# Attention block of a three-layer kernel: where the row factor of the input norm is multiplied in

## The chip, the cores and the metric

The kernel runs on one core of a Trainium2 chip. A core has five engines with a queue of instructions each, which run in order and wait for one another through semaphores: TensorE (PE, matrix products into the accumulator memory PSUM; the load of its stationary operand is listed as PEld), VectorE (DVE), ScalarE (ACT), GpSimd (POOL) and SyncE (SP, which here issues the DMAs). The metric is the device time of one execution in microseconds (us), the median over several runs. A profile is one further execution, taken with the hardware profiler.

## What is computed

Three transformer layers over 256 tokens of width 1024. The part that the change touches is the second norm of the first layer and the attention behind it, in the reference:

```python
x = x + FFN_RESIDUAL * rmsnorm(swiglu(rmsnorm(x, g[0]), ffn_w_in[i, 0], ffn_w_out[i, 0]), g[1])
h = rmsnorm(x, g[2])
...
m = diff_attention(h, attn_w_qkv[j], attn_w_o[j], attn_lam[j], attn_subln_g[j], rel_bias, lambda_init)
...
x = x + rmsnorm(m, g[3])
```

`rmsnorm(x, g)` is x times g (a weight per column) times the row factor 1/sqrt(mean of x squared + 1e-6), one number per token. `diff_attention` projects h to queries, keys and values, with 8 heads of 128 columns.

## The kernel before

**Data.** X, the residual stream, lies in SBUF with tokens on partitions, in two halves h = 0 and 1 of 128 tokens. A linear layer needs its input with columns on partitions, so the normed half `xn` is turned: eight PE transposes of 128x128 a half (`transposed`, line 2279), four to a PSUM bank. Products run in two-part precision: each operand is split into a rounded high part and the remainder. For the turned input ACT copies PSUM to `xhi` (`evict_hi`, line 822) and DVE subtracts to get `xlo` (`evict_lo`, line 1447). For weights, SP loads 1 MB pairs of units into `raw`, ACT writes `whi` (line 747), DVE writes `wlo` (line 1325). A unit is 128x1024 and four units are split at a time, so that `whi` of unit u waits until PE has used unit u-4. Each product is made of three: high times high, high times low, low times high (all on line 2134, where `mm` is).

**The place.** Unit 65 is the last of the first feed-forward layer (`ffn(0)`). Units 66 to 69 are the value weights `v0` of heads 0 to 3, units 70 and 71 the query and key weights of head 0, 72 and 73 those of head 1, and so on.

Between `ffn(0)` and `v0` the norm is settled, in an order that is written out by hand for each engine (`take_turns` with `ORDER_DEFER`, six steps for h = 0 woven with six for h = 1). For each half: ACT squares the layer's output with a row sum (`squares`, 787); POOL makes its row factor `r1` (610, 615); DVE multiplies by the weights g1 (1395, 1402) and adds to X (`add_x`, 1422); ACT squares X with a row sum (`squares2`, 814); POOL makes the second row factor `r2`; DVE writes `xn` = X times r2 times g2 (`norm`, 1430). Then PE turns `xn`. While PE waits it runs products whose result is not used: `fill_in` and `turn_idle`, twelve ahead of the first turn (`meanwhile`) and four ahead of the second, which stands in the middle of the v0 products of half 0 (`values`).

**Attention.** Head after head, PE runs the two query and key units (24 products each), the scores, the transposes of the softmax weights and the product with the values. The steps of different heads are interleaved by fixed lags (`head_at`). For each head, ACT takes queries and keys out of PSUM (`query_key`, 988 and 989), takes the exponential (964) and turns up again for three smaller steps; DVE adds the bias and takes the maximum (1593, 1596), weights the two softmaxes (1601 to 1612), scales the head's output (1620) and makes its low part (1626). All of that stands in the queues between the splits of the weight units (747, 1325).

Of the kernel before, what the change touches and what calls it, by code (L numbers as in the profile page):

```python
# [8 lines left out]
S = 256  # L9
# [22 lines left out]
DEFER = (1,)  # L32
# [3 lines left out]
FOLDED = STARTS + GATES  # L36
# [78 lines left out]
def n_sq(k, h, i=None):  # L115

    n = N_SQ1[k]
    if k in DEFER:
        return n_sq_first(k, h, i)
    i = n + 1 if i is None else i  # L120
    return n_sq_first(k, 0, 0) + (h * n + i if i < n else n + 2 * h + i)
# [64 lines left out]
def program(nc, w, rows, cols, pT, b1c, ssm_s, ssm_b, ssm_c, ssm_cc, oh, idn, eo, x, out, scr):  # L186
# [4 lines left out]
    with ctx:  # L191
# [85 lines left out]
        s_g8, s_vv, s_lam, s_lexp, s_qk = (sem(n) for n in ("s_g8", "s_vv", "s_lam", "s_lexp", "s_qk"))  # L277
# [67 lines left out]
        g8 = b1t[:, 128:256]  # L345
        lam, le = stat(4), stat(2)
# [256 lines left out]
        def gpsimd(g):  # L603
# [27 lines left out]
            def settle(k):  # L631
                if k in FOLDED or k == STORED:
# [100 lines left out]
        def scalar(a):  # L733
# [251 lines left out]
            def query_key(h):  # L985
                b = 4 + h % 2
                q.wait_ge(s_used, ATTN_AT + QK_AT[h] + 2)
                a.activation(turned(q_t[:, h, :]), in128(PS[:, b, 0:S]), ACT.Copy, scale=0.125)
                a.activation(k_t[:, h, :], PS[:, b, S:2 * S], ACT.Copy).then_inc(s_qk, 1)

            def values(name, bank, cols, out):
                for h in range(2):
# [4 lines left out]
                    a.activation(vv[:, h, out], PS[:, bank + h, cols], ACT.Copy).then_inc(s_vv, 1)  # L997

            def attention():
                def heads(j):  # L1000
                    for h in head_at(j, 4):
                        turned_weights(h)
                    for h in head_at(j, 0):
                        query_key(h)
# [7 lines left out]
                linear("v0", 4, head=4, tail=0, finish=lambda: evict_hi(1, 1))  # L1012
# [270 lines left out]
            settle(1, {1: lambda: released(0)})  # L1283
# [28 lines left out]
        def vector(v):  # L1312
# [91 lines left out]
            def add_x(k, h):  # L1404
# [12 lines left out]
                for i, f in enumerate((LO, HI)):  # L1417
# [4 lines left out]
                    v.scalar_tensor_tensor(X[:, h, f], src[:, f], by, X[:, h, f], MUL, ADD).then_inc(s_X, 1)  # L1422

# [203 lines left out]

            def attention():
                def heads(j):
                    for h in head_at(j, 6):  # L1630
                        head_normed(h)
# [10 lines left out]
                for j in range(4, 30):  # L1642
                    heads(j)
# [450 lines left out]
            take_turns(1, steps, {2: lambda: released(0)})  # L2094
# [34 lines left out]
        def tensor(pe):  # L2129
# [109 lines left out]
            def meanwhile(k, h):  # L2239
                b = tr_bank(k, h, 0)  # L2240
                if h and k not in DEFER:
# [8 lines left out]
                if k not in DEFER:  # L2250
                    turn_idle(k, b, s_X, n_x(k, 1, 1), 8 if k == PLACED else 4)

            def transposed(k, h):
# [3 lines left out]
                if k not in FOLDED and not (h and k in DEFER):  # L2257
                    meanwhile(k, h)
# [189 lines left out]
            def scores(h):  # L2448
                q.wait_ge(s_qk, h + 1)
# [32 lines left out]
            def attention():  # L2482
                def values(name, cols, bank, ns, last, by_half=None):
# [3 lines left out]
                    for h in range(2):  # L2487
# [614 lines left out]
```

## Time and profile before

| | us |
|---|---|
| median of 3 runs (1666.51 to 1667.78) | 1667.3 |
| the profiled execution | 1664.28 |
| its span, first to last instruction | 1662.5 |
| PE busy in the span | 1632.9 |
| DVE busy | 1101.2 |
| ACT busy | 927.6 |
| POOL busy | 165.8 |

PE is busy 98% of the span, but that counts the products whose result is not used. The settling of the attention's norm lies between 196 and 219 us of the span, the eight heads up to about 304 us. In the rows below a time such as 203.80 is in us from the start of the span.

### The profile page before, as it was taken

What the parts mean: (1) busy time and instruction counts of PE and PEld (TensorE: products, weight loads), DVE (VectorE), ACT (ScalarE), POOL (GpSimd) and SP (SyncE); (2) the same over time, 40 slices, a digit from 0 to 9 for tenths busy, and PEclk for the clock granted to TensorE, in tenths of its full rate; (3) what the DMA queues carried; (4) which work ended last, traced back from release to release, by engine and by line L of the source; (5) the groups of instructions that cost most, each with busy time, mean ns of one, the idle gap of its engine ahead of it and who ended that gap; (6) DMA issues with size and microseconds to landing.
All of it is one profiled execution on the core that took longest, in us unless ns stands there. A gap on an engine that the chain in (4) does not pass through costs nothing.

```text
span 1662.5 us, 22547 instructions
## 1 busy us (share of the span) xinstructions
PE 1632.9 (98%) x8995; PEld 1372.6 (83%) x8995; DVE 1101.2 (66%) x1567; ACT 927.6 (56%) x1559; POOL 165.8 (10%) x240
## 2 busy tenths in 40 slices
PE   9999999999999999999999999999999999999997
PEld 7888899788888877888878888788889889788886
DVE  5555667788877664869775556755567776665555
ACT  6555556655567585452465556655555444655555
POOL 0000001128301111900000000000000000000000
PEclk9999999999999999999999999999999999999999
DMA  6765443555555544451555545565544333554552
GB/s 235 252 209 186 181 165 127 179 195 191 189 191 190 206 174 152 174 181 52 190 184 182 198 178 190 192 219 199 179 176 178 140 116 128 184 203 177 196 184 102
DMA packets 50297, 295.93 MB, mean 178 GB/s; under 512 B 6072, under 2 KB 12688, under 8 KB 16528
## 3 DMA queue, kind: packets, MB, share of 16 engines
q1 hardware_dynamic: 49744, 293.86, 49.4%
q8 instruction: 71, 1.16, 0.3%
q0 software_dynamic: 160, 0.52, 0.1%
q14 instruction: 34, 0.28, 0.1%
q10 hardware_dynamic: 288, 0.11, 0.0%
HBM read 293.39 MB, written 1.09 MB: 177 GB/s over the span
## 4 chain that ended last, share of the span: by engine, by line
PE 89%; DVE 5%; ACT 4%; issue 1%; POOL 0%; DMA 0%; POOLq 0%; DVEq 0%; ACTq 0%
PE PS L2134 84%; PE PS L2356 2%; DVE wlo L1325 1%; PE PS L2279 1%; PE PS L2137 1%; ACT SC L964 1%; ACT whi L747 1%; PE PS L2571 0%; ACT wk L787 0%; DMA raw<-in_w 0%; DVE SC L1910 0%; DVE SC L1612 0%; DVE st L1596 0%; ACT wk L814 0%; DVE SC L1593 0%
## 5 line engine op out<-in xcount | busy, mean ns | idle before, releaser
L1331 DVE SCALAR_TENSOR_TENSOR wlo<-raw,ct,whi 128x512 fp32r<-128x512 f32 (+1 forms) x552 | 425.1, 815 | 259.2 <-ACT whi L751 259.2
L2134 PE MATMUL PS<-whi,xhi 128*128 128x512 f32 (+1 forms) x1312 | 505.6, 395 | 6.0 <-DVE wlo L1331 2.2
L751 ACT ACTIVATE whi<-raw,ct 128x512 fp32r<-128x512 f32 (+1 forms) x552 | 377.5, 734 | 224.2 <-PE PS L2134 170.6
L2134 PE MATMUL PS<-wlo,xhi 128*128 128x512 f32 (+1 forms) x1312 | 495.5, 387 | 0.0
L1325 DVE TENSOR_TENSOR wlo<-raw,whi 128x1024 fp32r<-128x1024 f32 x240 | 296.6, 1244 | 215.9 <-ACT whi L747 215.5
L2134 PE MATMUL PS<-whi,xlo 128*128 128x512 f32 (+1 forms) x1312 | 405.5, 387 | 0.0
L747 ACT ACTIVATE whi<-raw 128x1024 fp32r<-128x1024 f32 x240 | 251.8, 1057 | 258.4 <-PE PS L2134 192.1
L2134 PEld LDWEIGHTS PS<-whi,xhi 128*128 128x128 f32 x1312 | 246.0, 188 | 60.9 <-ACT xhi L822 4.1
L2134 PEld LDWEIGHTS PS<-whi,xlo 128*128 128x128 f32 x1312 | 246.4, 188 | 51.4
L2134 PEld LDWEIGHTS PS<-wlo,xhi 128*128 128x128 f32 x1312 | 246.6, 188 | 47.4
L2134 PE MATMUL PS<-whi,hhi 128*128 128x512 f32 x544 | 173.3, 392 | 0.1
L2134 PE MATMUL PS<-wlo,hhi 128*128 128x512 f32 x544 | 171.9, 389 | 0.0
L2134 PE MATMUL PS<-whi,hlo 128*128 128x512 f32 x544 | 171.6, 389 | 0.0
L610 POOL TENSOR_SCALAR st<-st 128x1 f32<-128x1 f32 x42 | 14.4, 343 | 1139.6 <-ACT wk L787 592.2
L2134 PE MATMUL PS<-xhi,whi 128*128 128x256 f32 x416 | 119.8, 289 | 0.0
L2134 PEld LDWEIGHTS PS<-whi,hlo 128*128 128x128 f32 x544 | 102.1, 188 | 21.4
L2134 PEld LDWEIGHTS PS<-wlo,hhi 128*128 128x128 f32 x544 | 102.1, 188 | 21.3
L2134 PEld LDWEIGHTS PS<-whi,hhi 128*128 128x128 f32 x544 | 101.0, 188 | 20.8 <-issue 0.7
L2134 PE MATMUL PS<-xhi,wlo 128*128 128x256 f32 x416 | 117.3, 283 | 0.0
L2134 PE MATMUL PS<-xlo,whi 128*128 128x256 f32 x416 | 116.4, 283 | 0.0
L881 ACT ACTIVATE wk<-PS,st 128x256 f32<-128x256 f32 x132 | 60.7, 470 | 41.4 <-PE PS L2134 40.6
L2134 PEld LDWEIGHTS PS<-xhi,whi 128*128 128x128 f32 x416 | 79.6, 191 | 1.6 <-issue 0.4
(282 smaller groups left out, 1508.7 us busy)
## 6 DMA issues: line engine op xcount, KB each, us to landing
raw<-in_w SPq DMA_DIRECT2D x263, 1024.0 KB, 4.8
gr<-in_rows SPq DMA_DIRECT2D x14, 512.0 KB, 3.9
SC<-scratch SPq DMA_DIRECT2D x5, 512.0 KB, 5.7
X<-in_x SPq DMA_DIRECT2D x2, 512.0 KB, 5.1
raw<-in_w SPq DMA_DIRECT2D x2, 512.0 KB, 6.7
SC<-scratch SPq DMA_DIRECT2D x4, 256.0 KB, 5.1
xn<-in_sc SPq DMA_DIRECT2D x2, 512.0 KB, 6.1
SC<-scratch SPq DMA_DIRECT2D x1, 1024.0 KB, 8.8
```

What stands on the lines that cost most here:

```text
L610: g.tensor_scalar(ms, ss[:, 0:1], ss[:, 1:2], eps, ADD, ADD).then_inc(s_ms, 1)
L747: a.activation(hi, src, ACT.Copy).then_inc(s_hi, 1)
L751: e = a.activation(hi[:, f], src[:, f], ACT.Copy, scale=ct[:, c:c + 1])
L881: a.activation(sg[:, h, :], PS[:, up_bank(n, j) + h, 0:S], ACT.Silu, scale=r2[k][h]).then_inc(s_silu, 1)
L964: e = a.activation(pr[:, m, l:z], sc[:, m, l:z], ACT.Exp, bias=n4[:, m, c:c + 1], accum_out=s4[:, m, c:c + 1])
L1325: v.tensor_tensor(lo, src, hi.bitcast(f32), SUB).then_inc(s_lo, 1)
L1331: e = v.scalar_tensor_tensor(lo[:, f], src[:, f], ct[:, c:c + 1], hi[:, f].bitcast(f32), MUL, SUB)
L2134: return pe.matmul(o, l, r, start=start, stop=stop)
L2137: return pe.matmul(o, l, r, start=False, stop=True, skip_group_check=True)
L2279: e = pe.transpose(PS[:, tr_bank(k, h, kq), 128 * i:128 * i + 128], src[:, h, 128 * (4 * kq + i):128 * (4 * kq + i) + 128], idt[:, :])
L2356: e = pe.transpose(PS[:, turn_bank(n), at:at + 128], hf[:, h, 128 * i:128 * i + 128], idt[:, :])
```

## The change

The row factor r2 is no longer multiplied into `xn`. What is turned is X times the weights g2 alone, and r2 is multiplied in later: into the values when ACT takes them out of PSUM (tokens are on partitions there, so r2 is ACT's scale per partition), and into queries and keys, where tokens are along the free axis and a row of factors is needed that is the same on all partitions. For that, DVE multiplies a 128x128 identity by r2 of each half (`factors`), PE transposes the two, DVE copies the result into `rk`, and `query_key`, which moves from ACT to DVE, multiplies by `rk` as it leaves PSUM. The idle products of this norm are gone. Half 1 is turned after all v0 products of half 0 rather than in their middle. `squares2` of both halves moves on ACT behind the eviction of half 1.

```diff
 def settle(k):
-    if k in FOLDED or k == STORED:
+    if k in FOLDED + DEFER or k == STORED:
...
-def query_key(h):
-    b = 4 + h % 2
-    q.wait_ge(s_used, ATTN_AT + QK_AT[h] + 2)
-    a.activation(turned(q_t[:, h, :]), in128(PS[:, b, 0:S]), ACT.Copy, scale=0.125)
-    a.activation(k_t[:, h, :], PS[:, b, S:2 * S], ACT.Copy).then_inc(s_qk, 1)
...
-        a.activation(vv[:, h, out], PS[:, bank + h, cols], ACT.Copy).then_inc(s_vv, 1)
+        q.wait_ge(s_r2, n_one(1, h))
+        a.activation(vv[:, h, out], PS[:, bank + h, cols], ACT.Copy, scale=r2[1][h]).then_inc(s_vv, 1)
...
+    def turned_1():
+        evict_hi(1, 1)
+        squares2(1, 0)
+        squares2(1, 1)
-    linear("v0", 4, head=4, tail=0, finish=lambda: evict_hi(1, 1))
+    linear("v0", 4, head=4, tail=0, finish=turned_1)
...
-settle(1, {1: lambda: released(0)})
+squares(1, 0)
+released(0)
+squares(1, 1, (0,))
+evict_hi(1, 0, (0,))
+squares(1, 1, (1,))
+use(ATTN_AT - 1)
+evict_hi(1, 0, (1,))
+use(ATTN_AT)
 attention()
...
+def add_x_times_g2(k, h):
+    q.wait_ge(l_x[h], 16)
+    q.wait_ge(s_r1, n_r1(k, h))
+    q.wait_ge(s_yg, n_yg(k, h))
+    g2 = row_in(ROW_G2[k])
+    for i, f in enumerate((LO, HI)):
+        v.scalar_tensor_tensor(X[:, h, f], yg_of(k, h)[:, f], r1[k][h], X[:, h, f], MUL, ADD).then_inc(s_X, 1)
+        q.wait_ge(s_X, n_x(k, h, i))
+        v.tensor_tensor(xn[:, h, f], X[:, h, f], g2[:, f], MUL).then_inc(s_xn, 1)
...
+def factors():
+    q.wait_ge(s_tr, n_tr(1, 1))
+    for h in range(2):
+        q.wait_ge(s_r2, n_one(1, h))
+        v.tensor_scalar(xn[:, h, 768:896], idt[:, :], 0.0, r2[1][h], MUL, ADD).then_inc(a_rk, 1)
+
+def query_key(h):
+    if h == 0:
+        q.wait_ge(a_rkT, 1)
+        v.tensor_copy(rk, PS[:, 2, 0:S].rearrange("p (h t) -> p h t", h=2)).then_inc(a_rk, 1)
+        q.wait_ge(a_rk, 3)
+    q.wait_ge(s_used, ATTN_AT + QK_AT[h] + 2)
+    b = PS[:, 4 + h % 2, :]
+    v.scalar_tensor_tensor(turned(q_t[:, h, :]), in128(b[:, 0:S]), 0.125, rk, MUL, MUL)
+    v.tensor_tensor(in128(k_t[:, h, :]), in128(b[:, S:2 * S]), rk, MUL).then_inc(a_key, 1)
...
 for j in range(4, 30):
+    if j == 5:
+        factors()
     heads(j)
...
-take_turns(1, steps, {2: lambda: released(0)})
+gate_or_low(1, 0)
+times_g(1, 0)
+add_x_times_g2(1, 0)
+released(0)
+evict_lo(1, 0, (0,))
+gate_or_low(1, 1)
+times_g(1, 1)
+use(ATTN_AT - 1)
+evict_lo(1, 0, (1,))
+use(ATTN_AT)
+add_x_times_g2(1, 1)
 attention()
...
-                if k not in FOLDED and not (h and k in DEFER):
+                if k not in FOLDED + DEFER:
                     meanwhile(k, h)
...
+                        if h and by_half is not None:
+                            transposed(1, 1)
-                            if low is False and h == 0 and n == 2:
-                                fill_in(tr_bank(1, 1, 0), ATTN_AT, 4)
-                                transposed(1, 1)
...
                 values("v0", slice(0, 512), 0, range(4), True, 1)
+                q.wait_ge(a_rk, 2)
+                for h in range(2):
+                    e = pe.transpose(PS[:, 2, 128 * h:128 * h + 128], xn[:, h, 768:896], idt[:, :])
+                e.then_inc(a_rkT, 1)
```

In the orders that follow, `PS` is PSUM, `PS<-whi` alone is a product whose result is not used, `SC` the scratch that holds queries, keys and softmax, `gr` the rows of norm weights, `idt` the identity. On PE, between the last product of `ffn(0)` and the first of v0, before:

```order
L2134 MATMUL PS<-whi,hlo 128x512
L2134 MATMUL PS<-whi 128x512 [waits s_lo,s_sq]
L2134 MATMUL PS<-whi 128x512 x3
L2134 MATMUL PS<-whi 128x512 [waits s_r1]
L2134 MATMUL PS<-whi 128x512 x3
L2134 MATMUL PS<-whi 128x512 [waits s_X]
L2134 MATMUL PS<-whi 128x512 x3
L2279 MATMUL PS<-idt,xn 128x128 [waits s_xn,s_vec]
L2279 MATMUL PS<-idt,xn 128x128 x3
L2279 MATMUL PS<-idt,xn 128x128 [waits s_xn]
L2279 MATMUL PS<-idt,xn 128x128 x3
L2134 MATMUL PS<-whi,xhi 128x512 [waits s_xhi]
```

And now:

```order
L2179 MATMUL PS<-whi,hlo 128x512
L2323 MATMUL PS<-idt,xn 128x128 [waits s_xn,s_vec]
L2323 MATMUL PS<-idt,xn 128x128 x3
L2323 MATMUL PS<-idt,xn 128x128 [waits s_xn]
L2323 MATMUL PS<-idt,xn 128x128 x3
L2179 MATMUL PS<-whi,xhi 128x512 [waits s_lo,s_xhi]
```

The twelve idle products are gone, and the turn of half 0 stands right behind the feed-forward layer.

On PE, between the last v0 product and the first query and key unit, before:

```order
L2134 MATMUL PS<-whi,xhi 128x512
L2134 MATMUL PS<-wlo,xhi 128x512
L2134 MATMUL PS<-whi,xlo 128x512
L2134 MATMUL PS<-xhi,whi 128x256 [waits s_lo]
L2134 MATMUL PS<-xlo,whi 128x256
```

And now:

```order
L2179 MATMUL PS<-whi,xlo 128x512
L2567 MATMUL PS<-idt,xn 128x128 [waits a_rk]
L2567 MATMUL PS<-idt,xn 128x128
L2179 MATMUL PS<-xhi,whi 128x256 [waits s_lo]
L2179 MATMUL PS<-xlo,whi 128x256
```

The two transposes of the factors are new there, with a wait for DVE's `factors`.

On DVE, from the end of the settling to the first head, before:

```order
L1447 TENSOR_TENSOR xlo<-PS,xhi 128x4x128 [waits s_xhi] x2
L1430 SCALAR_TENSOR_TENSOR xn<-X,st,gr 128x512 [waits s_r2]
L1430 SCALAR_TENSOR_TENSOR xn<-X,st,gr 128x512
L1640 TENSOR_SCALAR b1t<-b1t 128x128 [waits l_b1]
L1325 TENSOR_TENSOR wlo<-raw,whi 128x1024 [waits s_hi] x2
L1447 TENSOR_TENSOR xlo<-PS,xhi 128x4x128 [waits s_xhi] x2
L1325 TENSOR_TENSOR wlo<-raw,whi 128x1024 [waits s_hi] x6
```

And now:

```order
L1435 SCALAR_TENSOR_TENSOR X<-PS,st,X 128x512
L1437 TENSOR_TENSOR xn<-X,gr 128x512 [waits s_X]
L1673 TENSOR_SCALAR b1t<-b1t 128x128 [waits l_b1]
L1462 TENSOR_TENSOR xlo<-PS,xhi 128x4x128 [waits s_xhi] x2
L1330 TENSOR_TENSOR wlo<-raw,whi 128x1024 [waits s_hi] x4
L1647 TENSOR_SCALAR xn<-idt,st 128x128 [waits s_r2,s_tr]
L1647 TENSOR_SCALAR xn<-idt,st 128x128 [waits s_r2]
L1330 TENSOR_TENSOR wlo<-raw,whi 128x1024 [waits s_hi]
L1652 COPY xn<-PS 128x2x128 [waits a_rkT]
L1656 SCALAR_TENSOR_TENSOR SC<-PS,xn 128x2x128 [waits s_used,a_rk]
```

The two low parts of units 68 and 69 now stand further ahead, in the settling, and `factors` stands behind the low parts of units 70 to 73.

## Rows read from the trace of the kernel before

**Rows 1.** Waits of PE, whole span: waiter, releaser, us in total, times, longest.

```profile
PE PS L2819 <- DVE SC L2007: 3.6, 2, 1.9
...
PE PS L2465 <- DVE SC L1612: 0.8, 1, 0.8
PE PS L2465 <- DVE hlo L1626: 0.6, 1, 0.6
```

**Rows 2.** PE's timeline, 200 to 220: start, us, instruction, count, idle before, releaser.

```profile
200.35 2.88 PE L2134 MATMUL PS<-whi 128*128 128x512 f32 x12
203.80 1.23 PE L2279 MATMUL PS<-idt,xn 128*128 128x128 f32 x8 [0.57 <-DVE xn L1430]
...
208.95 1.32 PE L2279 MATMUL PS<-idt,xn 128*128 128x128 f32 x8
210.88 0.50 PE L2134 MATMUL PS<-whi,xhi 128*128 128x512 f32 x1 [0.61 <-DVE wlo L1325]
...
219.39 0.28 PE L2134 MATMUL PS<-xhi,whi 128*128 128x256 f32 x1
```

**Rows 3.** DVE's timeline in the same stretch.

```profile
198.44 1.41 DVE L1422 SCALAR_TENSOR_TENSOR X<-PS,st,X 128x512 f32<-128x512 f32 x2 [0.40 <-POOL st L615]
...
208.14 1.41 DVE L1430 SCALAR_TENSOR_TENSOR xn<-X,st,gr 128x512 f32<-128x512 f32 x2 [1.31 <-POOL st L615]
...
209.61 2.35 DVE L1325 TENSOR_TENSOR wlo<-raw,whi 128x1024 fp32r<-128x1024 f32 x2
...
219.38 2.52 DVE L1325 TENSOR_TENSOR wlo<-raw,whi 128x1024 fp32r<-128x1024 f32 x2 [0.19 <-ACT whi L747]
```

**Rows 4.** ACT's timeline in the same stretch.

```profile
204.46 1.20 ACT L822 ACTIVATE xhi<-PS 128x512 fp32r<-128x512 f32 x2 [2.19 <-PE PS L2279]
205.55 0.62 ACT L814 ACTIVATE wk<-X 128x512 f32<-128x512 f32 x1
...
206.36 0.63 ACT L814 ACTIVATE wk<-X 128x512 f32<-128x512 f32 x1
...
206.99 1.99 ACT L747 ACTIVATE whi<-raw 128x1024 fp32r<-128x1024 f32 x2
...
219.59 1.06 ACT L747 ACTIVATE whi<-raw 128x1024 fp32r<-128x1024 f32 x1 [0.24 <-PE PS L2134]
```

**Rows 5.** PE's timeline inside the heads: two small transposes and the product behind them.

```profile
251.37 0.44 PE L2479 MATMUL PS<-idt,xn 128*128 128x128 f32 x2
251.56 0.36 PE L2134 MATMUL PS<-xhi,whi 128*128 128x256 f32 x1
```

**Rows 6.** ACT's timeline inside the heads: queries and keys, twice.

```profile
255.42 0.38 ACT L988 ACTIVATE SC<-PS 128x256 f32<-128x256 f32 x1
255.68 0.39 ACT L989 ACTIVATE SC<-PS 128x256 f32<-128x256 f32 x1
...
286.38 0.39 ACT L988 ACTIVATE SC<-PS 128x256 f32<-128x256 f32 x1 [1.02 <-PE PS L2134]
```

**Rows 7.** DVE's timeline inside the heads, one head of the steady run.

```profile
257.13 0.60 DVE L1620 SCALAR_TENSOR_TENSOR xn<-PS,st,b1t 128x128 f32<-128x128 f32 x2
258.97 1.23 DVE L1325 TENSOR_TENSOR wlo<-raw,whi 128x1024 fp32r<-128x1024 f32 x1 [1.23 <-ACT whi L747]
```

**Rows 8.** DVE instructions from PSUM by line: ns min/median/max, first and last start, forms.

```profile
L1509 DVE SCALAR_TENSOR_TENSOR wk<-PS,st,wk x132: 466/479/486, 28.1 to 1613.6; 128x256 f32<-128x256 f32 x132
...
L1626 DVE TENSOR_TENSOR hlo<-PS,hhi x4: 412/414/417, 253.8 to 277.6; 128x256 fp32r<-128x256 f32 x4
```

**Rows 9.** PE's timeline at the start and at the end of the span.

```profile
1.04 5.49 PE L2134 MATMUL PS<-rot 128*128 128x128 f32 x24 [1.04 <-DVE rot L2089]
...
7.59 2.84 PE L2134 MATMUL PS<-rot 128*128 128x128 f32 x24
...
1653.05 0.39 PE L2134 MATMUL PS<-whi,xlo 128*128 128x512 f32 x1
```

**Rows 10.** Stretch, its length, busy PE, PEld, DVE, ACT, POOL; granted clock, DMA share, GB/s.

```profile
1655.50:1656.00 0.50, 0.00 (x0) 0.00 (x0) 0.50 (x1) 0.41 (x2) 0.29 (x1) 0.74 0.00 0
```

More of the change, by code:

```diff
@@ L117, in n_sq @@
     n = N_SQ1[k]
-    if k in DEFER:
-        return n_sq_first(k, h, i)
     i = n + 1 if i is None else i
@@ L276, in program @@
         s_phi, s_plo, s_prj, s_gate, s_gated = (sem(n) for n in ("s_phi", "s_plo", "s_prj", "s_gate", "s_gated"))
-        s_g8, s_vv, s_lam, s_lexp, s_qk = (sem(n) for n in ("s_g8", "s_vv", "s_lam", "s_lexp", "s_qk"))
+        a_rk, a_rkT, a_key = (sem(n) for n in ("a_rk", "a_rkT", "a_key"))
+        s_g8, s_vv, s_lam, s_lexp = (sem(n) for n in ("s_g8", "s_vv", "s_lam", "s_lexp"))
         a_sc, a_add, a_max, a_exp, a_rc, a_at, a_pt, a_aT, a_av, a_sq, a_r, a_on, a_xt, a_oh, a_ol = (
@@ L345, in program @@
         g8 = b1t[:, 128:256]
+        rk = xn[:, :, 896:1024]
         lam, le = stat(4), stat(2)
@@ L1002, in heads @@
                         turned_weights(h)
-                    for h in head_at(j, 0):
-                        query_key(h)
                     for h in head_at(j, 7):
@@ L1626, in head_lo @@
                 v.tensor_tensor(lo, PS[:, o_bank(h), 0:S], hi.bitcast(f32), SUB).then_inc(a_ol, 1)
+            def factors():
[12 more added lines that the diff above has]
+                v.tensor_tensor(in128(k_t[:, h, :]), in128(b[:, S:2 * S]), rk, MUL).then_inc(a_key, 1)
             def attention():
                 def heads(j):
+                    for h in head_at(j, 0):
+                        query_key(h)
                     for h in head_at(j, 6):
@@ L2240, in meanwhile @@
                 b = tr_bank(k, h, 0)
-                if h and k not in DEFER:
+                if h:
                     if k == PLACED:
@@ L2249, in meanwhile @@
                 turn_idle(k, b, s_X, n_x(k, h, 1), 9 if k == PLACED else 4)
-                if k not in DEFER:
-                    turn_idle(k, b, s_X, n_x(k, 1, 1), 8 if k == PLACED else 4)
+                turn_idle(k, b, s_X, n_x(k, 1, 1), 8 if k == PLACED else 4)
             def transposed(k, h):
@@ L2448, in scores @@
             def scores(h):
-                q.wait_ge(s_qk, h + 1)
+                q.wait_ge(a_key, h + 1)
                 if h:
@@ L2528, in attention @@
                     if h >= 2:
-                        q.wait_ge(s_qk, h - 1)
+                        q.wait_ge(a_key, h - 1)
                     for n in range(2):
@@ L2535, in attention @@
                     heads(22 + n)
-                q.wait_ge(s_qk, 8)
+                q.wait_ge(a_key, 8)
                 linear("wo", o_place, 4, tail=2, step=-2, ready=lambda k: q.wait_ge(a_ol, k + 1),
```

## The prediction, made before the changed kernel was run

> **What bounds the kernel now.** I read the waits of PE first. In the whole attention only two waits of PE are worth naming, both at the turn of a head's softmax weights: 0.8 us behind DVE L1612 and 0.6 us behind DVE L1626 [rows 1]. Elsewhere in the heads PE runs without a gap, so PE's own time is the bound there, and what the change can win lies at the settling of the norm. There I read the timelines of three engines side by side. PE is free of the feed-forward layer at 200.35, runs idle products, waits for xn, turns half 0 at 203.80, half 1 at 208.95, waits again until 210.88 for a low part of weights, and starts the first query and key unit at 219.39 [rows 2]: 19.0 us. Of that, 48 v0 products are real work; the 36 from 210.88 to 219.39 take 8.51 us, 0.236 each, some 11 us for all, and the two turns take 2.6 [rows 2]. So some 5.4 us are waiting or idle products. The price is the chain X, squares, r2 on POOL, then xn: DVE stands 1.31 us for r2 even at half 1 [rows 3].
>
> **The change part by part.** I follow the new orders with the durations of the rows, in the old span's time.
>
> Half 0. X starts at 198.44 as before, since r1 is unchanged. Two X halves back to back take 1.41 [rows 3], one alone some 0.74. The new X times g2 on 128x512 is not in the trace; it lies between half of a 128x1024 subtraction (2.35/2/2 = 0.59) and one of the L1430 pair (0.70) [rows 3]; I take 0.65, nearer the form with two tensors. With the wait for its own X each pair costs some 1.45, so the second half of xn is done at 201.3 and PE has turned half 0 at 202.1. Before, that was 203.80 + 1.23 = 205.0 [rows 2]. Gain so far 2.9 us.
>
> DVE then becomes the bound, since everything stands in one queue: low part of unit 67 (1.17), xlo (0.65), two multiplications by g1 (0.65 each), low part of unit 68 (1.17), xlo (0.65), low part of unit 69 (1.17): 201.3 + 6.1 = 207.4. PE needs unit 69 for the last quarter of half 0 and ends that at some 209.3. X and xn of half 1 take 2.9 more on DVE: 210.2. The turn of its second bank (0.65), ACT's xhi (1.20/2 = 0.60 [rows 4]) and xlo bring PE to 211.4, and 24 products of half 1 end at 216.9. Before it was 219.39 [rows 2]. Gain 2.5 us, with 1.5 to 3.3 as bounds, by how many of the nine DVE steps overlap.
>
> The factors. Here the change adds a wait that the diff hardly shows. PE's two new transposes stand ahead of the first query and key unit and wait for `factors`; `factors` stands on DVE behind the low parts of units 70 to 73; unit 73 needs ACT's high part, and that waits until PE has used unit 69, the last v0 unit. So PE waits for something that only begins when PE has finished. Before, ACT took unit 73 at 219.59, 0.20 after v0 ended, and DVE ended its low part at 219.38 + 2.52 = 221.90, 2.51 after it [rows 3, 4]; nobody waited for that. Two `factors` add some 0.36 and the start of PE 0.14: at least 3.0 us.
>
> It is more, since ACT comes late: behind the eviction of half 1 (211.4) stand four `squares2`, 0.81 each by their starts (206.36 - 205.55), 3.2 us, and then four high parts at 1.0 [rows 4]: 211.4 + 3.2 + 4.0 = 218.6. DVE follows: first low part from 215.7, four at 1.17, 220.4, `factors` 220.7, PE 220.9. The transposes cost 0.19 (251.37 to 251.56) and some 0.1 on the product behind them [rows 5]. First unit at 221.1 instead of 219.39: the settling is **1.7 us slower**, not faster; bounds +0.8 and +2.5. Behind the waiting transposes stands all of PE's work.
>
> The r2 that values and factors need is there by some 215.8 and holds nobody. SP passes its wait for the last xn at some 210.2 instead of 209.5 and its next weight pair is wanted at 216.6, so the loads stay hidden. Values with a scale cost ACT nothing that PE sees.
>
> Queries and keys. ACT loses 0.65 us per head (255.42 to 256.07) [rows 6]. DVE gains one multiplication like L1509, 0.48, and one like L1626, 0.41 [rows 8], some 0.8 back to back, 6.4 for eight heads. In the steady head DVE is done with L1620 at 257.73 and stands 1.23 us until ACT's high part releases 258.97 [rows 7]. The 0.8 stand right in front of L1620, so that gap hides them, with 0.4 to spare. If the cover were gone, each head would cost up to 0.8. A page bears on this: the Trainium skill, VectorE: DVE Perf Modes, Specifications, says that VectorE sits closer to SBUF and ScalarE closer to PSUM, which speaks against moving a PSUM read to DVE. The rows show little of it, 0.41 and 0.48 on DVE against 0.38 and 0.39 on ACT [rows 6, 8], and the sum goes by the rows.
>
> What the heads give back. The 0.6 us at L2465 came from a loop of ACT and DVE (exponential, high part, low part, softmax weights, bias, maximum) that ran as tight as PE. With PE 1.7 us later against it and ACT shorter, that wait should go. The 0.8 us came from ACT standing 1.02 us for the queries of the last head ahead of an exponential [rows 6]; with DVE doing those, the exponential starts some 0.6 earlier and 0.15 of the wait is left. Together **-1.2 us**, bounds 0 and -1.4. What is late next is PE itself.
>
> The clock. The wait of PE at the factors is some 3.9 us (216.9 to 220.9), and the idle products that used to fill this settling are gone. The longest waits of PE inside the trace are 1.9 us [rows 1], and no stretch of the work shows the granted clock below full. At the end, PE's last product ends at 1653.44 and the granted clock falls from 1.0 (2.4 GHz) to half in the middle of 1655.5 to 1656.0, 2.3 us later [rows 9, 10]. So a wait of 3.9 us is past what PE got away with and past what it did not. What a fall costs I bound by the start of the span: 24 idle products took 5.49 us there and the next 24 took 2.84 [rows 9]: 0 to 2.65 us lost, and I take 1.4, the middle. The Trainium skill, TensorE: Matmul & The Clock Gate, HAM oscillation, says the same in general: gaps in PE's work throttle it to half rate, and it has to be busy again before it is released. By that page alone the fall would be counted in full, and the sum would be its upper end, +3.2; this trace shows the fall once, at the end, and the return only by the durations at the start.
>
> **Sum** against the profiled 1664.28: +1.7 - 1.2 = +0.5 if the clock holds, 1664.8; +1.9 with the fall, 1666.2. The median of the runs stands 3.0 above the profiled execution; carried over, 1667.8 and 1669.2.
>
> **The rivals.** What a measurement here can tell from no change is about 0.2%, 3.3 us.
> (a) Forecast: the wait at the factors eats the gain and the clock falls: +1.9, 1669.2. For it: 3.9 us of wait against 2.3 us at the end. Against it: the fall needs to meet the wait, and I have one instance.
> (b) The same with the clock held: +0.5, 1667.8. For it: all waits inside the trace passed without a fall. Against it: they were half as long.
> (c) Slower beyond 0.2%: DVE becomes the bound of the heads. Place: DVE between L1620 and the low part of the even unit, gap 1.23 against 0.8 [rows 7]. It decides once the query and key pair takes over 1.23, say from the reversed write of queries, or if the 0.4 to spare is used up by late units; then the loop of ACT and DVE lengthens by up to 0.8 a head, 6.4 in all, less the 1.2 not given back: with (a), +3 to +8, 1672 as its middle. Against it: both forms are in the rows at half the gap.
> (d) Faster: the wait at the factors is short because v0 ends late or ACT early, and the gain of the settling is at its upper bound: -3.3 + 3.2 - 1.4 = -1.5 at best as a sum of rows, and beyond -3.3 only if the transposes didn't wait. The order says that they do. 1665.8 for the first, 1663 for the second.
>
> **How the numbers follow.** (a) 0.48, (b) 0.35, (c) 0.10, (d) 0.07, of which 0.05 go beyond -3.3. The likeliest is (a): 1669.2. The range takes (a) and (b) with their bounds: lowest +0.8 - 1.4 without a fall, -0.6, and some 1 us for the spread of the runs (1666.51 to 1667.78): 1665.7; highest +2.5 + 2.65 less 0.6 of the give-back, +4.5: 1671.8; what lies outside is most of (c) and half of (d). Faster 0.05; slower 0.13, (c) and a corner of (a); same 0.82.
>
> **What would show it.** Right: PE's first turn in attention ends near 202, v0 ends near 217, then PE idles 3 to 4 us with DVE's L1647 as releaser; the granted clock is below 1 in a few us around 221; in the heads L2465 no longer waits, and DVE's gap ahead of the even low part shrinks to some 0.4. Wrong: PE waits in every head behind DVE L1656 or L1657 (c); no wait at L2567 (d); the clock at 1.00 throughout (b).

## The result, and the profile after

The changed kernel takes 1667.25 us (median of 21 runs), the kernel before takes 1664.54 beside it (21 runs): ratio 1.0016, 95% interval 1.001 to 1.0021, some 2.7 us slower. That is within the 0.2% that the prediction counts as no change, and near its forecast of +1.9. The kernel before is 2.8 us quicker here than in the three runs from which the prediction started (1667.3; they are among the 21, and among the slower ones), so differences are compared below, not times. The profiled execution of the changed kernel is the slowest of its runs (1669.09, span 1667.3); what stands in its trace is not all typical, and a second profile is used beside it. One execution of a later run (factors first), at 2330 us, was a slow one and is left out of its ratio and of the counts below.

TensorE's timeline at the settling, as in [rows 2] (start, us, instruction, count, idle before, releaser):

```profile
201.16 0.66 PE L2323 MATMUL PS<-idt,xn 128*128 128x128 f32 x4 [0.41 <-DVE xn L1437]
201.57 0.48 PE L2179 MATMUL PS<-whi,xhi 128*128 128x512 f32 x1
...
205.31 0.47 PE L2179 MATMUL PS<-whi,xhi 128*128 128x512 f32 x1 [0.74 <-DVE wlo L1330]
...
206.95 0.50 PE L2179 MATMUL PS<-whi,xhi 128*128 128x512 f32 x1 [0.47 <-DVE wlo L1330]
...
211.03 0.47 PE L2179 MATMUL PS<-whi,xhi 128*128 128x512 f32 x1 [0.64 <-ACT xhi L822]
...
216.36 0.39 PE L2179 MATMUL PS<-whi,xlo 128*128 128x512 f32 x1
220.51 0.44 PE L2567 MATMUL PS<-idt,xn 128*128 128x128 f32 x2 [3.76 <-DVE xn L1647]
220.70 0.36 PE L2179 MATMUL PS<-xhi,whi 128*128 128x256 f32 x1
```

Half 0 is turned at 201.8 where it was 205.0, and the last v0 product starts at 216.36. Then TensorE stands for 3.76 us, the longest wait of its whole trace (the two transposes at 220.51), and the first query and key unit starts at 220.70 where it was 219.39. (The feed-forward layer ends at 200.15 here and 200.35 there, so 0.2 comes on top.) What it waits for is seen on ScalarE and VectorE, whose timelines answer to [rows 4] and [rows 3]. ScalarE:

```profile
213.98 1.99 ACT L747 ACTIVATE whi<-raw 128x1024 fp32r<-128x1024 f32 x2
216.61 2.00 ACT L747 ACTIVATE whi<-raw 128x1024 fp32r<-128x1024 f32 x2 [0.64 <-DMA raw<-in_w]
```

VectorE:

```profile
215.05 2.36 DVE L1330 TENSOR_TENSOR wlo<-raw,whi 128x1024 fp32r<-128x1024 f32 x2 [3.32 <-ACT whi L747]
217.70 2.36 DVE L1330 TENSOR_TENSOR wlo<-raw,whi 128x1024 fp32r<-128x1024 f32 x2 [0.28 <-ACT whi L747]
219.97 0.48 DVE L1647 TENSOR_SCALAR xn<-idt,st 128x128 f32<-128x128 f32 x2
```

The factors (L1647) stand on VectorE behind four low parts, and these follow four high parts that ScalarE begins at 213.98. The second pair of them waits 0.64 us for its load.

In a steady head VectorE now has the queries and keys (L1656, L1657) in the gap of [rows 7], and 0.57 us of the gap is left:

```profile
257.80 0.42 DVE L1656 SCALAR_TENSOR_TENSOR SC<-PS,xn 128x256 f32<-128x256 f32 x1
258.13 0.41 DVE L1657 TENSOR_TENSOR SC<-PS,xn 128x256 f32<-128x256 f32 x1
258.46 0.60 DVE L1635 SCALAR_TENSOR_TENSOR xn<-PS,st,b1t 128x128 f32<-128x128 f32 x2
259.64 1.23 DVE L1330 TENSOR_TENSOR wlo<-raw,whi 128x1024 fp32r<-128x1024 f32 x1 [0.57 <-ACT whi L747]
```

Among TensorE's waits there is none of the kind of [rows 1] at L2465 any more.

**Where the time goes, place by place.** For each profile I took the end of the feed-forward layer on TensorE (the row behind its last product: 200.35 before, 200.15 after) as zero, and from its timeline the start of the first query and key unit and of four later rows that every kernel has. Two of these rows, of after and then of before:

```profile
324.17 0.50 PE L2179 MATMUL PS<-whi,xhi 128*128 128x512 f32 x1 [0.25 <-ACT xhi L822]
...
802.81 0.73 PE L2179 MATMUL PS<-whi,xhi 128*128 128x512 f32 x2 [0.46 <-DVE xlo L1827]
```

```profile
324.12 0.50 PE L2134 MATMUL PS<-whi,xhi 128*128 128x512 f32 x1 [0.25 <-ACT xhi L822]
...
801.62 0.73 PE L2134 MATMUL PS<-whi,xhi 128*128 128x512 f32 x2 [0.45 <-DVE xlo L1792]
```

So at 324 the changed kernel is (324.17 - 200.15) - (324.12 - 200.35) = 0.25 us behind, at 802 it is 1.39 behind. The table gives that difference from the kernel before for all profiles of the study, in us (plus is later). The names of the runs are explained with the experiments.

| profile | first query unit, 220 | end of attention, 324 | 802 | 1308 | 1437 |
|---|---|---|---|---|---|
| before again | 0.00 | -0.02 | -0.17 | -0.17 | -0.17 |
| after | +1.51 | +0.25 | +1.39 | +1.41 | +5.02 |
| after again | +1.77 | +2.04 | +3.15 | +3.15 | +3.30 |
| turn later (e1) | -2.64 | -3.21 | -2.10 | -2.08 | +0.21 |
| factors first (e6) | -2.47 | -3.34 | -2.26 | -2.22 | -0.33 |
| idle in wait (e4) | +1.67 | +0.44 | +0.33 | +0.32 | +1.84 |
| idle in wait again | +1.55 | +0.30 | +0.15 | +0.16 | +0.12 |
| code only (e9) | +2.89 | +2.86 | +2.78 | +3.68 | +3.66 |
| factors first, padded (e8) | -2.47 | -3.18 | -3.21 | -3.18 | -1.67 |
| e8 again | -2.51 | -3.30 | -3.19 | -3.19 | -0.40 |
| idle in sliding (e11) | -2.49 | -3.17 | -3.26 | -2.60 | +1.61 |
| three idle (e12) | -2.51 | -3.35 | -3.34 | -3.35 | -3.35 |
| before, three idle (e13) | +0.02 | 0.00 | -0.09 | -0.14 | -0.18 |

Read the row of after from left to right: 1.5 us behind at the settling, 1.26 of it given back in the heads, then 1.1 us lost between 324 and 802, in code that the change does not touch, and 3.6 us lost in the third layer. Of these 3.6, 2.8 lie on two stretches at half clock behind 1309 and 1365, and 0.8 on a late load at 1435. The attention alone does not explain the result. What follows asks for each of these steps whether it belongs to the change.

### The profile page after: what moved, and what is told of

The parts are those of the page before. It is cut to its first block, busy times and chain, and to the rows that moved or that the text cites. A ratio compares the mean times of both kernels' runs of the same rounds, so it can differ in the third digit from the quotient of the medians.

```text
span 1667.3 us, 22526 instructions
## 1 busy us (share of the span) xinstructions
PE 1633.2 (98%) x8981; PEld 1372.5 (82%) x8981; DVE 1105.8 (66%) x1586; ACT 923.0 (55%) x1543; POOL 165.7 (10%) x240
## 3 DMA queue, kind: packets, MB, share of 16 engines
q8 instruction: 71, 1.16, 0.3%
## 4 chain that ended last, share of the span: by engine, by line
PE 89%; DVE 5%; ACT 3%; DMA 2%; issue 1%; POOL 0%; POOLq 0%; DVEq 0%; ACTq 0%; SPq 0%
PE PS L2179 84%; DMA raw<-in_w 2%; PE PS L2400 2%; DVE wlo L1330 1%; PE PS L2182 1%; PE PS L2323 1%; DVE wlo L1336 1%; ACT whi L747 1%; PE PS L2618 0%; ACT wk L787 0%; DVE SC L1945 0%; ACT whi L751 0%; DVE SC L1948 0%; ACT xhi L822 0%; DVE SC L2115 0%
```

## The experiments

All edits are in the changed kernel unless it is said otherwise. Ratios are to the kernel before, run beside it; they stand as the record gives them and can differ from the quotient of two medians by 0.0005.

### Is the factors' wait on the path? (e1, e6) And which losses come again? (two second profiles)

Turn later, on TensorE:

```diff
-q.wait_ge(a_rk, 2)
-for h in range(2):
-    e = pe.transpose(PS[:, 2, 128 * h:128 * h + 128], xn[:, h, 768:896], idt[:, :])
-e.then_inc(a_rkT, 1)
 for h in range(8):
+    if h == 1:
+        q.wait_ge(a_rk, 2)
+        for m in range(2):
+            e = pe.transpose(PS[:, 2, 128 * m:128 * m + 128], xn[:, m, 768:896], idt[:, :])
+        e.then_inc(a_rkT, 1)
```

> TensorE turns the two factors of the keys only after head 0's two query/key units, instead of ahead of them; nothing else is changed. Theory A (the 3.76 us of idle ahead of the first of these transposes in the changed kernel lie on the path that sets the end): the idle row with the releaser L1647 goes or falls under 0.3 us, the first query/key unit starts near 216.9 us of the span instead of 220.7, and the time falls by 3 to 3.9 us against the changed kernel, so to 1.0 to 1.6 us under the kernel before (ratio 0.9992). Theory B (the attention is held by VectorE or ScalarE and the wait only moves on): the first unit starts earlier, but its second or the scores wait for most of it, and the time stays within 1 us of the changed kernel (ratio 1.0010 to 1.0020).

Factors first, on VectorE:

```diff
 for j in range(4, 30):
-    if j == 5:
+    if j == 4:
         factors()
```

> VectorE makes the factors of the keys one slot earlier, ahead of the low parts of the last four weight units of the values; the order on TensorE stays. Theory A (VectorE's factors come late only because they stand behind those low parts in its order): the idle of TensorE ahead of the two small transposes falls from 3.76 to about 0.2 us, and the time falls by about 3.5 us against the changed kernel (ratio to before 0.9995). Theory B (the factors come late since their sums of squares come late from ScalarE, at 213.9 us): the idle stays above 2 us or moves to the first query/key unit, which then waits for the low parts, and the time falls by under 1.5 us (ratio 1.0007 or more).

Turn later takes 1663.45 us, ratio 0.9996 (0.9987 to 1.0005); factors first 1664.22, ratio 1.0004 (0.9994 to 1.0013); the changed kernel beside them 1667.22. Both are theory A: 3.0 to 3.8 us less by the medians, 3.5 and 3.6 at the end of the attention by the table. In factors first the two instructions run ahead of the low parts, and TensorE doesn't wait at all. VectorE, then TensorE:

```profile
212.50 0.29 DVE L1647 TENSOR_SCALAR xn<-idt,st 128x128 f32<-128x128 f32 x1 [1.84 <-POOL st L615]
214.05 0.29 DVE L1647 TENSOR_SCALAR xn<-idt,st 128x128 f32<-128x128 f32 x1 [1.26 <-POOL st L615]
214.25 4.77 DVE L1330 TENSOR_TENSOR wlo<-raw,whi 128x1024 fp32r<-128x1024 f32 x4
```

```profile
215.27 0.39 PE L2179 MATMUL PS<-whi,xlo 128*128 128x512 f32 x1
215.50 0.38 PE L2567 MATMUL PS<-idt,xn 128*128 128x128 f32 x2
```

The row factors are there at 214.05, in an idle time of VectorE. So what made the wait was the place of `factors` behind the low parts of units 70 to 73, not when the factors could be made.

> The changed kernel once more, for a second profile and more times. If the 2.7 us of the medians' difference are the attention's own, the alignment of TensorE's products with the kernel before shows +2.5 us or more at the end of the attention. If they come from the third layer (two stretches of some 3.4 us at granted clock 0.5, near 1311 and 1366 us, and loads that land late near 696 and 1431 us), the attention shows +0.3 us again, and the same stretches are there again at the same places. If these were of one execution alone, they are at other places or absent, and the span is 3 to 4 us shorter than 1667.3.

> The kernel before once more, for a second profile. If stretches at granted clock 0.5 in the third layer belong to the changed kernel, there are none ahead of 1655 us here, as in the first profile of it (span 1662.5). If they belong to an execution, not to a kernel, they can appear here too, and the span is longer by 1.2 to 1.7 us for each.

The second profile of the changed kernel (1667.22 us, ratio 1.0018, 1.0009 to 1.0027) decides between the steps. The 1.1 us between 324 and 802 are there again (from +2.04 to +3.15), and in turn later and factors first too (from -3.21 to -2.10, from -3.34 to -2.26): they come with the change. Of the 3.6 us of the third layer only 0.15 are there. Instead the attention ends at +2.04 rather than +0.25, for TensorE's granted clock, of which the first profile shows nothing there (stretch, its length, busy time, granted clock, DMA share, GB/s; first after, then after again):

```profile
219.00:220.50 1.50, 0.00 (x0) 1.00 0.86 350
220.50:222.00 1.50, 1.49 (x13) 1.00 1.00 393
```

```profile
219.50:220.00 0.50, 0.40 (x4) 0.99 0.97 410
220.00:223.00 3.00, 3.00 (x17) 0.50 0.92 360
```

In the second profile the transposes come after 4.02 us of idle, and from 220 to 223.5 the products run at granted clock 0.50, that is 1.2 GHz: 17 in 3 us where 13 took 1.5. With after's give-back of 1.26 the end of the attention would be at +0.51; it is at +2.04, so the fall costs 1.5 us. The profiles of before show no such stretch ahead of the end, in either (that this does not hold for all executions of before is seen at the end of the experiments).

### What is late between 324 and 802? (e4, e9)

The place is one load of weights in the first layer's second feed-forward. ScalarE waits for it. Its timeline before:

```profile
690.64 2.01 ACT L747 ACTIVATE whi<-raw 128x1024 fp32r<-128x1024 f32 x2 [4.24 <-DMA raw<-in_w]
```

After, where the same step starts 1.56 us later:

```profile
692.20 2.01 ACT L747 ACTIVATE whi<-raw 128x1024 fp32r<-128x1024 f32 x2 [5.74 <-DMA raw<-in_w]
```

TensorE, 5 us further on, waits for what follows from it; before, it has no wait there:

```profile
697.27 0.70 PE L2179 MATMUL PS<-whi,hhi 128*128 128x512 f32 x2 [0.83 <-DVE hlo L1530]
```

The load is issued at 685.9 before and 686.0 after, and lands 4.7 us later before and 6.2 after. The difference stands in the DMA queues. This is the view of the queues before, from 683 to 686, when no load is moving (queue, packets, MB, share of 16 engines):

```profile
q8 instruction: 1, 0.02, 2.1%
```

and after, from 686 to 692 (first the busy share of the 16 DMA engines in 40 slices):

```profile
DMA  0000009900000999999999999990300000101000
...
q1 hardware_dynamic: 144, 1.05, 54.4%
q8 instruction: 1, 0.02, 1.0%
```

Queue q8 brings code: 71 packets, 1.16 MB in the span, against 0.28 MB on q14, and TensorE has 17,962 of the 22,526 instructions (products and weight loads), so q8 is most likely TensorE's. Before, the packet comes at 684.6, between two loads. After, TensorE has 14 products and their 14 weight loads fewer, the packet comes at 689.4 and takes 0.93 us on one of the 16 DMA engines, in the middle of the load's transfer. A few packets of the load end late: see the three stray marks behind the block of nines. That they are the share of the DMA engine that carried the code is my reading; the view doesn't tell the 16 engines apart. The Trainium skill, Runtime: NRT & Kernel Launch, Instruction fetch mechanics, says that code comes in blocks of 16 KiB and that crossing one is mostly hidden. The size agrees (1.16 MB in 71), and TensorE itself runs on without a gap around 689.4. What pays is the load that the packet meets.

To test it, idle in wait gives TensorE 14 products back, where they cost no time:

```diff
+fill_in(3, ATTN_AT + 4, 14)
 q.wait_ge(a_rk, 2)
 for h in range(2):
     e = pe.transpose(PS[:, 2, 128 * h:128 * h + 128], xn[:, h, 768:896], idt[:, :])
```

> Into the changed kernel's wait for the two factor transposes (3.76 and 4.02 us in its two profiles) go 14 idle products of TensorE (128x512, 0.23 us each, 3.2 us in all), about as many as the change took out ahead of the first turn; the rest stays. Two theories on what makes the changed kernel 2.7 us slower at the median while its attention alone shows +0.24 us where the granted clock holds. Code theory: with 28 instructions fewer on TensorE, its code (fetched in packets of 16 KB) arrives at other times, and the packet at 689.4 us of the span, 0.93 us long, falls into the transfer of a weight load and holds one of its 16 parts back (landing 1.4 us late, TensorE idle 0.83 us at 697 us, +1.1 us in each profile of the three kernels that have the change); with the 28 instructions given back the packet moves to about 685 to 686, ahead of that load's transfer, the idle at 697 goes, and the time falls by about 1.1 us. Clock theory: the idle wait also drops the granted clock in part of the executions (half clock from 219.8 to 223.4 us in one of the two profiles, +1.5 us); with the idle products it holds there, and the median falls by up to 1.5 us more. Both together: ratio to before 1.0000 to 1.0007. If neither holds: 1.0014 to 1.0020, with the idle at 697 us still there.

> The changed kernel with the 14 idle products in its wait once more, for a second profile: if the idle products hold the clock, no half clock between 219 and 224 us again, and TensorE's idle at 697 us is absent again, since the code is the same.

Measured: 1665.11 us, ratio 1.0000 (0.9991 to 1.0009), and once more 1665.14, 1.0000 (0.9990 to 1.0010). The lag behind the kernel before is gone. For the code's part of it the mechanism named is seen. The view of the queues from 683 to 686 has the code packet again:

```profile
q8 instruction: 1, 0.02, 2.4%
```

ScalarE's high part comes at its old place,

```profile
690.15 2.01 ACT L747 ACTIVATE whi<-raw 128x1024 fp32r<-128x1024 f32 x2 [4.42 <-DMA raw<-in_w]
```

TensorE has no wait at L1530 in this stretch, and from 324 to 802 the table shows -0.11 and -0.15 instead of +1.1. Only TensorE's queue was edited, so the load's delay hangs on TensorE's instruction count. All 14 profiles bear this out. In the time of the kernel before (the packet's time less the lag at 324 and the shift of the zero) the packet stands at 688.8 to 689.4 in the four that lose the 1.1 us (after twice, turn later, factors first) and at 684.4 to 685.2 in the ten that don't. The clock held at 220 in both profiles of idle in wait.

The same is there once more in the third layer. ScalarE, before and then after:

```profile
1427.66 2.01 ACT L747 ACTIVATE whi<-raw 128x1024 fp32r<-128x1024 f32 x2 [4.25 <-DMA raw<-in_w]
```

```profile
1432.97 2.01 ACT L747 ACTIVATE whi<-raw 128x1024 fp32r<-128x1024 f32 x2 [5.58 <-DMA raw<-in_w]
```

The code packet that comes at 1420.8 before comes in the same time at 1426.2 after and 1426.5 in turn later, into the load, and TensorE loses 0.8 us in each from 1431 to 1437. In factors first and after again it comes at 1423.7, and the loss is 0.46 and 0.12. None of the other profiles loses anything there. So the count of instructions costs the changed kernel 1.1 us at 697 and 0.1 to 0.8 at 1435.

Two things were changed by that run, the code's place and the empty wait. Code only gives the 14 products (256 columns, 0.12 us each) to three short waits inside the values' unit and leaves the long one empty:

```diff
+PADS = {(0, 2): 5, (0, 3): 4, (1, 0): 5}
...
+if by_half is not None and low is not True and (h, n) in PADS:
+    for _ in range(PADS[h, n]):
+        p = weight(LAST[name] - 3)[0]
+        mm(PS[:, 4, 0:256], p[:, 0:128], p[:, 0:256], True, True)
```

> The changed kernel with the 14 idle products of 256 columns in the three short waits of the values' unit (as in the run factors first, padded), and with the factors where the changed kernel makes them: TensorE's code moves as in the run idle in wait, but the wait of 3.8 us ahead of the factor transposes stays empty. This tells the two parts of that run's 2.4 us apart. Code theory for 1.1 us of it: the idle of 0.83 us at 697 us is gone. Clock theory for the rest: the empty wait still drops the granted clock in part of the executions, so the time stays 1 to 1.6 us above the run idle in wait (ratio to before 1.0006 to 1.0011). If the code alone were the cause, 1.0000 to 1.0004; if the clock alone, 1.0014 or more.

Measured: 1667.22 us, ratio 1.0020 (1.0011 to 1.0029). The time is that of "the clock alone", and taken by itself it speaks against the code. The trace says otherwise: the loss between 324 and 802 is gone (-0.08), but the attention ends 2.86 us behind. Another code packet, at 214.6 us, now falls into the load that ScalarE needs for units 72 and 73. It waits 1.87 us for that load instead of 0.64, the factors' wait grows to 5.02 us, and the half clock follows. (That this packet meets the load is a matter of the execution: e8 again, with the same code there, waits 1.88 us for this load, and the profiles of e8, e11 and e12 wait 0.68 to 0.72.) ScalarE, TensorE, and two stretches of TensorE:

```profile
216.65 2.00 ACT L747 ACTIVATE whi<-raw 128x1024 fp32r<-128x1024 f32 x2 [1.87 <-DMA raw<-in_w]
```

```profile
220.54 0.69 PE L2573 MATMUL PS<-idt,xn 128*128 128x128 f32 x2 [5.02 <-DVE xn L1647]
```

```profile
221.00:222.00 1.00, 1.00 (x7) 0.50 0.78 147
222.00:223.00 1.00, 1.00 (x7) 0.50 0.96 401
```

So the run did not separate the two parts by its time. It shows the same collision in a second place, with a price of 1.0 to 1.3 us (5.02 against 4.02 and 3.76), and the half clock a second time behind an empty wait. How much of idle in wait's gain (some 2.7 us by the ratios) is code and how much is clock is told only by the profiles: 1.1 to 1.3 us code at 697, in every one, and 0.1 to 0.8 at 1435; the rest would be the clock. In this profile 0.9 us more are lost between 802 and 1308, at 1052, where TensorE waits for nothing that the profile shows; I have no cause for it.

### Both causes taken away (e8), and the third layer's clock (e11, e12, e13)

Factors first, padded is factors first with the 14 products of code only. As TensorE doesn't wait for the factors there, a late load at 214 does not reach it: e8 again, where ScalarE waits 1.88 us for it, starts its first unit no later than e8 (-2.51 and -2.47).

> VectorE makes the factors one slot earlier (as in the run factors first), and 14 idle products of 256 columns (0.12 us each) go into three waits that TensorE has in the values' unit anyway (0.74, 0.48 and 0.63 us): 5, 4 and 5 of them. Code theory: the attention keeps the gain of 3.3 us against the kernel before, the idle of 0.83 us at the L1530 wait in the first layer's feed-forward goes (1.1 us), and the time is 2.5 to 3.5 us under the kernel before (ratio 0.9979 to 0.9986, lower where the granted clock also holds in the third layer). If the late load there has another cause: it stays, and the ratio is that of the run without these products, 0.9996 to 1.0004.

> The kernel of the run factors first, padded, once more, beside the one with the idle products. If the half clock after the wait at 1305 us belongs to this kernel's order, it is there again; if it is the execution's, it is absent or at another of the waits (1361 us), and the span goes down by 1.3 us where it is absent.

Measured: 1661.88 us, ratio 0.9982 (0.9974 to 0.9991), and again 1660.76, 0.9976 (0.9966 to 0.9986). The attention's gain of 3.2 to 3.3 us against the kernel before now lasts until 1308 in both profiles. In the third layer each then loses: one stretch at half clock at 1306 to 1309 in the first, two, at 1305 and 1360, in the second, each right behind a wait of 1.7 to 1.9 us for the sliding attention's weights ([rows 1], L2819). So it was no trait of this kernel's order that makes it come at one place. All stretches at half clock between 8 and 1650 us, in the 14 profiles:

| where | waits empty | half clock behind them |
|---|---|---|
| ahead of the factors, 3.8 to 5.0 us | 3 profiles (after twice, code only) | 2 |
| the same, filled or without a wait | 8 profiles | 0 |
| third layer, two waits of 1.7 and 1.9 us | 11 profiles, 22 waits | 8; none in the 4 waits of before |
| the same, filled (e11, e12, e13) | 3 profiles | 0 |

Idle in sliding fills these waits:

```diff
+for _ in range(5):
+    mm(PS[:, 7, 0:256], aq[0:64, j, 128:256], ak[0:64, :], True, True)
 q.wait_ge(w_p, 2 * j + 2)
```

> To the kernel of the run factors first, padded, five idle products (fp32, 64 rows of the array, 256 columns, about 0.23 us each, 1.2 us in all) are added ahead of each of the four transposes of the third layer's sliding attention, where TensorE waits 1.68 to 1.88 us for the normalised weights in every kernel of this study. Clock theory (a profile of each kernel with the change shows a stretch of some 3.5 us at granted clock 0.5 that begins right after one of the long idle waits of TensorE, at 220, 1309 or 1361 us, +1.3 to +1.5 us each; the kernel before shows none in two profiles): with these waits filled, no half clock between 1290 and 1400 us, and the time falls by 1.2 to 1.5 us (ratio to before 0.9972 to 0.9976). Rival (the stretches are not tied to the idle time, or the idle products delay the transposes): half clock there again, or the transposes 0.2 us late each, and 0.9980 to 0.9986.

Measured: 1665.37 us, ratio 1.0000 (0.9991 to 1.0008), 4.6 us slower than e8 beside it, though no half clock is left. Both expectations miss. I had taken 0.23 us for a product and all four transposes for waiting ones. One such fp32 product took 0.48 and shows as two instructions (10 for five products), so five took 2.42 us, more than the wait, which is gone from the row behind them; and ahead of the second and fourth transposes there is no wait to fill:

```profile
1301.63 2.42 PE L2179 MATMUL PS<-SC 64*128 64x256 f32 x10
1303.99 0.88 PE L2874 MATMUL PS<-idt,SC 128*128 128x128 f32 x6
```

Three idle mends both (`range(0 if j % 2 else 3)`), and the last run puts the same products into the kernel before.

> As the run idle in sliding, but with three idle products instead of five (they took 0.48 us each there, so 1.45 us, under the 1.68 and 1.87 us of the waits) and only ahead of the first and third of the four transposes: ahead of the other two TensorE had no wait, so that five products cost their whole 2.4 us there. Clock theory: no half clock between 1290 and 1400 us, the transposes in their old places, and 1.3 to 2.7 us less than the kernel of the run factors first, padded (ratio to before 0.9962 to 0.9972). Rival: half clock there in spite of the idle products, or the time stays at 0.9976 to 0.9982.

> The kernel before with the same three idle products ahead of the same two transposes of the third layer. Its two profiles show no half clock there, although TensorE waits 1.68 and 1.88 us in the same two places. If its other executions don't have it either, the products change nothing (ratio 0.9997 to 1.0003); if part of its executions have it (its times spread over 5 us), the median falls by up to 1.5 us (ratio 0.9991 to 0.9997).

TensorE's timeline at the first of the two waits, three idle:

```profile
1302.93 1.56 PE L2179 MATMUL PS<-SC 64*128 64x256 f32 x6
1304.69 0.77 PE L2874 MATMUL PS<-idt,SC 128*128 128x128 f32 x5 [0.19 <-DVE SC L2042]
```

Measured: 1660.13 us, ratio 0.9975 (0.9966 to 0.9984); the kernel before with them 1663.18, 0.9997 (0.9988 to 1.0006). The profile is as the clock theory says: no half clock, and 3.35 us ahead of the kernel before from the attention to the end. But the median is no better than e8's two (0.9982 and 0.9976) by more than the intervals, where 1.3 to 2.7 us were expected. That no half clock follows filled waits is what three profiles show.

The timed executions can be asked too, since each has its mean granted clock on record. In the 14 profiles this mean is 0.999 only where there is no stretch at half clock inside, and 0.997 only where there is at least one; 0.998 can be either. Counted so (one of the 32 of after reads 0.946, at 1669.5 us):

| kernel | executions | 0.999 | 0.998 | 0.997 or less |
|---|---|---|---|---|
| before, beside the experiments | 115 | 44 | 35 | 36 |
| after, both times | 32 | 0 | 19 | 13 |
| turn later, factors first | 21 | 1 | 14 | 6 |
| idle in wait, both times | 19 | 7 | 4 | 8 |
| code only | 11 | 0 | 1 | 10 |
| factors first, padded, both times | 20 | 8 | 5 | 7 |
| third layer filled (e11, e12, e13) | 33 | 18 | 15 | 0 |

So the kernel before has falls as well, in about a third of its executions at least, and those take 2 us longer (1665.9 against 1663.7 in the mean); its two profiles happened to show none. With the third layer's waits filled, no execution of 33 is at 0.997. The fill does what it was meant to, but the gain in time is small: in the means, against the kernel before, 4.0 us with it and 3.1 and 3.7 without it, so it stays open between 0 and some 1 us. The table also bears on the clock ahead of the factors. Code only, with that wait empty, is at 0.997 or less in 10 of 11 executions, and idle in wait, with it filled, in 8 of 19. But turn later and factors first have no such wait, and they too are at 0.999 only once in 21: the falls of the kernels with TensorE's shorter queue can't be put down to the factors' wait alone.

Three idle is the fastest kernel of the study, 3.6 us by the medians under the kernel before and some 7 under the changed one.

## Why the prediction was right, and where it was not

**The settling.** Half 0 turned "near 202": 201.8. v0 done "near 217": 216.75. TensorE then idle "3 to 4 us with L1647 as releaser": 3.76 and 4.02. First unit "221.1 instead of 219.39", +1.7: +1.51 and +1.77. ScalarE's four high parts done at 218.6 by the sum, 218.6 in the trace; that they agree to a tenth is luck, as the next paragraph says. The size of the wait held because it was followed around its whole circle, v0 to high part to low part to factors.

**"So the loads stay hidden."** Not quite: the second pair of high parts waited 0.64 and 0.89 us for its load. The high parts began at 213.98 where the sum had 214.6, and lost the 0.64 again to the load: two misses that cancel. Code only shows that this load is at the edge: 1.2 us later and TensorE waits longer.

**The heads.** Give-back -1.2 forecast, -1.26 measured (+1.51 at the first unit, +0.25 at 324). The queries and keys on VectorE are hidden, as forecast, with 0.57 us left where the sum had 0.4. That they cost nothing rests on the trace; the run that was to test it, with both done twice in each head (+1 to +3.2 us expected), gave no time.

**The clock.** Forecast as the likeliest, +1.4, and "1.00 throughout" named as what would prove (b). The first profile shows 1.00 there, and the second shows the fall, 1.5 us. It is both (a) and (b), by execution: 2 of 3 profiles with the empty wait fell, none of 8 without it. The step was sound in mechanism and price, and wrong in kind: a fall behind a wait is something that part of the executions have. My argument from [rows 1] that the 1.9 us waits are what TensorE "got away with" is refuted: behind such waits the clock fell in 8 of 22 cases, and the kernel before itself falls in about a third of its timed executions. One profile without falls told nothing about the next execution.

**What the sum lacked.** +0.5 if the clock holds, at the end of the attention: +0.25 in the profile where it held. But then +1.1 us at 697, which no step of the prediction has. I counted the idle products that were taken out as time and as cover for the clock; they are also code, and 28 instructions fewer on TensorE moved its code packets (from 684.6 to 689.4, from 1420.8 to 1423.7 or later in the time of the kernel before), with 0.1 to 0.8 us more lost at 1435. Of this the profile before had shown all that was needed but the result: q8 in the list of queues, its packets' times, and loads that take 4.7 us from issue to landing and are issued every 4 to 8.

So the median's +2.7 us goes together as +0.25 in the attention, +1.1 and 0.1 to 0.8 by the two code packets, and a rest of 0.5 to 1.3 that is most likely the clock, since a fall costs 1.3 to 1.5 us and the executions of the changed kernel are never at 0.999. Whether these falls come ahead of the factors or in the third layer is not separated by any run. The forecast of +1.9 came near partly by luck: one term was missing (the code) and one, the fall, was counted in full for a single place. Its absolute time, 1669.2, also carries the 3.0 us by which three runs stood above the profile; over 21 runs that is 0.3.

**The rivals.** (b), the clock held at the factors, is one of the two profiles. (c), VectorE as the bound of the heads, did not come: no wait of TensorE behind L1656 or L1657. (d), faster, needed the transposes not to wait; e1 and e6 show that the price of that was one line, and e8, with the code padded too, keeps 3.2 us until the third layer.

## What to carry to other kernels

Where a small result is put into an engine's queue, look at what stands ahead of it there and not at when its inputs are ready: the factors could be made at 214.05 and were made at 219.97, and one line moved up was worth 3.5 us. An edit that changes the number of an engine's instructions can move its code packets in later stages, so an edit's effect is to be read stage by stage, and a loss in code that was not touched is first looked for in the DMA queues. Idle products are worth their place only if they fit the wait: fill it from measured durations of that very form, or they cost their whole time. How often the clock falls is not told by one or two profiles; the mean granted clocks of all timed executions tell it better.

## What the runs showed that I had not expected

One packet of TensorE's code, 16 KB and 0.93 us on one of 16 DMA engines, delayed the landing of a 1 MB load by 1.5 us (4.7 to 6.2 us), and TensorE lost 1.1 us by it; the same in a second place cost 1.0 to 1.3. Behind waits of 1.7 to 1.9 us the granted clock fell to 0.50 (1.2 GHz) in 8 of 22 cases, at 1.3 to 1.5 us a time, and a wait of 3.76 us passed at 1.00. The mean granted clock of the timed executions showed more of this than the profiles did. An fp32 product of 64 rows with 256 columns shows as two instructions of 0.24 us each, twice in all what I had put down for it.
